# First expert: the fifth unit's parts made before the rows' copies and the gates, the gate by tanh, the slot marks turned by TensorE and copied by ScalarE

## The reference

```python
def moe_swiglu(h, w_router, b_router, w_gate, w_up, w_down):
    t = h.reshape(n_tok, d)                              # 256 x 1024
    logits = (t @ w_router) + b_router                   # 8 experts
    top_v, top_e = lax.top_k(logits, TOP_K)              # TOP_K = 2
    gate = jax.nn.softmax(top_v, axis=-1)
    ...                                                  # rows sorted by expert
    def one(args):                                       # D_FF_EXPERT = 3584
        xb, e = args
        return (jax.nn.silu(xb @ w_gate[e]) * (xb @ w_up[e])) @ w_down[e]
    ...
    y = zeros.at[row_tok].add(out * row_g[:, None])
```

## Time and profile before

| | us |
|---|---|
| median of 3 runs | 2670.47 |
| lowest and highest | 2667.81, 2671.71 |
| the profiled execution's own time | 2667.92 |
| its span | 2666.1 |

### The profile page before, as it was taken

How to read it: one execution, slowest core, us unless ns; L and a number is a source line. 1 busy time by engine, 2 the same in 40 slices (tenths; PEclk the granted TensorE clock), 3 DMA queues, 4 the chain that set the end, 5 groups by cost and what they waited for, 6 DMA issues and landing times.

```text
span 2666.1 us, 65659 instructions
## 1 busy us (share of the span) xinstructions
PE 2564.8 (96%) x27832; PEld 2159.6 (81%) x27832; DVE 1957.1 (73%) x1886; ACT 1614.5 (61%) x1688; POOL 378.9 (14%) x440
## 2 busy tenths in 40 slices
PE   9999999999999999999999999999999999999998
PEld 8887788888887888898788888789777687786775
DVE  5467575565567765666775566798999999999997
ACT  4345664353356654455654445657888787888876
POOL 3214022122115222103022103031000000000000
PEclk9999999999999999999999999998999999999999
DMA  8574365555554555654465665478999999999996
GB/s 270 169 208 131 104 198 197 168 188 189 163 152 152 192 176 178 197 166 141 138 200 200 174 197 166 123 261 338 410 420 422 418 411 422 415 419 418 411 421 274
DMA packets 354985, 666.18 MB, mean 250 GB/s; under 512 B 24545, under 2 KB 285825, under 8 KB 315825
## 3 DMA queue, kind: packets, MB, share of 16 engines
q1 hardware_dynamic: 353920, 661.39, 68.9%
q0 software_dynamic: 528, 0.63, 0.3%
q10 hardware_dynamic: 288, 0.59, 0.1%
HBM read 661.49 MB, written 1.05 MB: 249 GB/s over the span
## 4 chain that ended last, share of the span: by engine, by line
PE 60%; DVE 20%; DMA 7%; ACT 6%; issue 4%; DVEq 2%; POOLq 0%; ACTq 0%; SPq 0%; POOL 0%
PE ps L2331 17%; PE ps L2333 17%; PE ps L2332 17%; DVE w_lo L1619 7%; DMA w<-in_moe_units 3%; DVE w_lo L1459 3%; DVE work L1619 2%; DVE ff L1619 2%; DMA mix<-in_moe_units 2%; ACT w_hi L955 2%; ACT w_hi L846 2%; DMA squares_and_low<-in_moe_units 1%; PE ps L2374 1%; PE ps L2380 1%; PE ps L2375 1%
## 5 line engine op out<-in xcount | busy, mean ns | idle before, releaser
L2331 PE MATMUL ps<-x_hi,w_hi 128*128 128x96 f16 (+2 forms) x5024 | 1077.0, 246 | 26.5 <-DVE w_lo L1619 6.6
L2333 PE MATMUL ps<-x_hi,w_lo 128*128 128x96 f16 (+2 forms) x5024 | 1076.3, 246 | 5.2 <-issue 5.1
L2332 PE MATMUL ps<-squares_and_low,w_hi 128*128 128x96 f16 (+2 forms) x5024 | 1076.4, 246 | 5.0 <-issue 4.9
L1459 DVE SCALAR_TENSOR_TENSOR w_lo<-w,w_hi 128x2048 f16<-128x2048 f32 (+3 forms) x335 | 693.9, 2082 | 295.1 <-ACT w_hi L846 293.4
L846 ACT ACTIVATE w_hi<-w 128x2048 f16<-128x2048 f32 (+3 forms) x335 | 556.8, 1671 | 85.6 <-PE ps L2333 74.8
L2331 PEld LDWEIGHTS ps<-x_hi,w_hi 128*128 128x128 f16 x5024 | 493.1, 98 | 82.8 <-issue 22.0
L2332 PEld LDWEIGHTS ps<-squares_and_low,w_hi 128*128 128x128 f16 x5024 | 492.8, 98 | 51.8 <-issue 7.0
L2333 PEld LDWEIGHTS ps<-x_hi,w_lo 128*128 128x128 f16 x5024 | 492.8, 98 | 48.4 <-issue 6.2
L2332 PE MATMUL ps<-ff,w_hi 128*128 128x272 f16 (+1 forms) x880 | 243.3, 276 | 0.0
L2333 PE MATMUL ps<-ff,w_lo 128*128 128x272 f16 (+1 forms) x880 | 243.3, 276 | 0.0
L2331 PE MATMUL ps<-ff,w_hi 128*128 128x272 f16 (+1 forms) x880 | 243.3, 276 | 0.0
(11 more groups left out here) (408 smaller groups left out, 4772.7 us busy)
## 6 DMA issues: line engine op xcount, KB each, us to landing
w<-in_ffn_w_up_units SPq DMA_DIRECT2D x176, 512.0 KB, 4.6
w<-in_moe_units SPq DMA_DIRECT2D x75, 1024.0 KB, 12.0
w<-in_moe_units SPq DMA_DIRECT2D x56, 1280.0 KB, 15.5
w<-in_w_in SPq DMA_DIRECT2D x112, 512.0 KB, 4.7
mix<-in_moe_units SPq DMA_DIRECT2D x50, 1024.0 KB, 12.0
mix<-in_moe_units SPq DMA_DIRECT2D x36, 1280.0 KB, 15.7
w<-in_mix_w_in SPq DMA_DIRECT2D x60, 512.0 KB, 4.9
squares_and_low<-in_moe_units SPq DMA_DIRECT2D x26, 1024.0 KB, 11.9
```

The source lines that it names most:

```text
L1459: vec.scalar_tensor_tensor(k.w_lo[:, s, 0:size], k.w32[:, s, 0:size], WS, k.w_hi[:, s, 0:size], ALU.mult, ALU.subtract).then_inc(k.parts_r ...
L2331: pe.matmul(acc, w_hi, x_hi, start=first, stop=False)
L2332: pe.matmul(acc, w_hi, x_lo, start=False, stop=False)
L2333: return pe.matmul(acc, w_lo, x_hi, start=False, stop=last)
```

## The change

Four edits, all for the first expert (the later rounds, which run only when an expert has over 96 tokens, follow suit):

- ScalarE makes unit 4's high part ahead of `take_high` instead of between the two copies.
- VectorE makes unit 4's low part right behind unit 3's, ahead of the gates; the gate is made from Tanh(x / 2) by two multiply-adds instead of from Exp by an addition, a reciprocal and a product. ScalarE loads Silu's table ahead of the Tanh.
- The turned marks are no longer made from spread ranks: TensorE turns `to_slot` itself by 16 matmuls with the identity (`turn_marks`, behind unit 3), and ScalarE copies the 96 x 2048 result (`take_marks`, at its step 5). `spread_ranks`, `take_ranks`, `sel16` and the constant `slot_col` go.
- GpSimd loads 14 constants instead of 15.

```diff
-RANKS_SPREAD, RANKS_TAKEN, GATES_SUMMED, GATES_TAKEN, SUM_BEGUN = 1, 3, 9, 11, 15
+MARKS_TURNED, MARKS_TAKEN, GATES_SUMMED, GATES_TAKEN, SUM_BEGUN = 3, 5, 9, 11, 15
-N_CONST = 15
+N_CONST = 14
...
+            if first and u == MARKS_TAKEN:
+                take_marks(0)
...
+    def take_marks(r):
+
+        act.wait_ge(k.marks_turned, r + 1)
+        act.activation(k.to_token[0:CAP, 1:1 + EXPERTS, :], halves(k.ps[0:CAP, TURNED[r]:TURNED[r] + 4, :]), ACT.Copy).then_inc(k.choice_ready, 1)
+
+    expert_split(0, 4, 0)
     take_high(0, 0)
-    expert_split(0, 4, 0)
     take_low(0, 2)
-    act.activation(k.warm2[:, :], k.eps[:, 0:1], ACT.Exp)
+    act.activation(k.warm[:, :], k.eps[:, 0:1], ACT.Silu)
     act.wait_ge(k.lg_ready, 1)
-    act.activation(k.rt[:, :, 1], k.rt[:, :, 0], ACT.Exp).then_inc(k.lg_exped, 1)
-    act.activation(k.warm[:, :], k.eps[:, 0:1], ACT.Silu)
+    act.activation(k.rt[:, :, 1], k.rt[:, :, 0], ACT.Tanh, scale=0.5).then_inc(k.lg_exped, 1)
...
-    vec.tensor_tensor(k.sel[:, :, :], k.member[:, :, :], ranks, ALU.mult)
-    vec.tensor_tensor(k.sel16[:, :, :], k.member[:, :, :], ranks, ALU.mult).then_inc(k.sel_ready, 1)
+    vec.tensor_tensor(k.sel[:, :, :], k.member[:, :, :], ranks, ALU.mult).then_inc(k.sel_ready, 1)
...
-    for u in range(3, E_AHEAD):
+    for u in range(3, E_AHEAD + 1):
         expert_split(0, u, 0)
...
-        vec.tensor_scalar(k.rt[:, :, 2], k.rt[:, :, 1], 1.0, None, ALU.add)
-        vec.drain()
-        vec.reciprocal(k.rt[:, :, 3], k.rt[:, :, 2])
-        vec.drain()
-        vec.tensor_tensor(k.rt[:, :, 4], k.rt[:, :, 1], k.rt[:, :, 3], ALU.mult)
+        vec.tensor_scalar(k.rt[:, :, 3], k.rt[:, :, 1], -0.5, 0.5, ALU.mult, ALU.add)
+        vec.tensor_scalar(k.rt[:, :, 4], k.rt[:, :, 1], 0.5, 0.5, ALU.mult, ALU.add)
...
-    def take_ranks(r):
-        vec.wait_ge(k.sel_spread, r + 1)
-        vec.tensor_scalar(k.to_token[:, 1:1 + EXPERTS, :], halves(k.ps[:, SPREAD[r]:SPREAD[r] + 4, :]), -float(CAP * r), k.slot_col[:, 0:1],
-                          ALU.add, ALU.is_equal).then_inc(k.choice_ready, 1)
...
-            if first and u == RANKS_TAKEN:
-                take_ranks(0)
...
-    def spread_ranks(r):
-
+    def turn_marks(r):
+
+        pe.wait_ge(k.slots_marked, r + 1)
         for e in range(EXPERTS):
             for t in range(2):
-                a = pe.matmul(k.ps[:, SPREAD[r] + e // 2, (e % 2) * T2 + t * P:(e % 2) * T2 + (t + 1) * P],
-                              k.sel16[:, t, e:e + 1].broadcast_to([P, P]), k.ident16[:, :], start=True, stop=True)
-        a.then_inc(k.sel_spread, 1)
+                a = pe.matmul(k.ps[0:CAP, TURNED[r] + e // 2, (e % 2) * T2 + t * P:(e % 2) * T2 + (t + 1) * P],
+                              k.to_slot[:, t, e, :], k.ident16[:, :], start=True, stop=True)
+        a.then_inc(k.marks_turned, 1)
...
-            if first and u == RANKS_SPREAD:
+            if first and u == MARKS_TURNED:
                 pe.wait_ge(k.ident16_made, 1)
-                spread_ranks(0)
+                turn_marks(0)
             if first and u == GATES_SUMMED:
                 pe.wait_ge(k.gates_split, 1)
-                pe.wait_ge(k.slots_marked, 1)
                 sum_gates(0)
```

More of the change, by code:

```diff
@@ L92 @@
 SUM_ADDED = 1
-SPREAD = (4, 0, 0)
+TURNED = (4, 0, 0)
 ROWS_BANK, LOGITS_BANK, ROW_SUMS_BANK, RANKS_BANK, FILLER_BANK = 4, 0, 1, 3, 2
 FILLERS = 4
-RANKS_SPREAD, RANKS_TAKEN, GATES_SUMMED, GATES_TAKEN, SUM_BEGUN = 1, 3, 9, 11, 15
+MARKS_TURNED, MARKS_TAKEN, GATES_SUMMED, GATES_TAKEN, SUM_BEGUN = 3, 5, 9, 11, 15
 GATE_SCALE = 2.0 ** 14
@@ L493, in allocate @@
     k.sel = sb("sel", [P, 2, EXPERTS], F32)
-    k.sel16 = sb("sel16", [P, 2, EXPERTS], F16)
     k.gates16 = sb("gates16", [P, 2, EXPERTS, 2], F16)
@@ L501, in allocate @@
     k.slots = sb("slots", [P, P], F32)
-    k.slot_col = sb("slot_col", [P, 1], F32)
     k.ms = sb("ms", [P, 2, 5], F32)
@@ L621, in allocate @@
     k.sel_ready = sem("sel_ready")
-    k.sel_spread = sem("sel_spread")
+    k.marks_turned = sem("marks_turned")
     k.first_marked = sem("first_marked")
@@ L1418, in moe_round @@
             expert_split(r, u, r * EXPERTS)
+        take_marks(r)
         take_high(r * EXPERTS, 0)
@@ L2071, in vec_program @@
     split_gates()
-    def take_ranks(r):
-        vec.wait_ge(k.sel_spread, r + 1)
-        vec.tensor_scalar(k.to_token[:, 1:1 + EXPERTS, :], halves(k.ps[:, SPREAD[r]:SPREAD[r] + 4, :]), -float(CAP * r), k.slot_col[:, 0:1],
-                          ALU.add, ALU.is_equal).then_inc(k.choice_ready, 1)
     def take_gates(r):
-        sums = k.ps[:, SPREAD[r], :]
+        sums = k.ps[:, TURNED[r], :]
         vec.wait_ge(k.gates_summed, r + 1)
@@ L2118, in take, with split_rest @@
                                          k.d_hi[0:CAP, :], ALU.mult, ALU.subtract).then_inc(k.down_ready, 1)
-        expert_units(lambda u: expert_split(r, u, q), take, last)
+        def split_rest(u):
+            if not (first and u == E_AHEAD):
+                expert_split(r, u, q)
+        expert_units(split_rest, take, last)
     for e in range(EXPERTS):
@@ L2130, in moe_round @@
         for e in range(EXPERTS):
-            mark(e, r)
-        take_ranks(r)
+            a = mark(e, r)
+        a.then_inc(k.slots_marked, 1)
         take_gates(r)
@@ L2230, in pool_program @@
                  (k.slots[:, :], i["c_slots"].broadcast_to([P, P])),
-                 (k.slot_col[:, :], i["c_slots"].rearrange("a s -> s a")),
                  (k.rb[:, :], i["moe_b_router_2"].broadcast_to([P, EXPERTS])),
@@ L3023, in sum_gates @@
             for t in range(2):
-                a = pe.matmul(k.ps[0:CAP, SPREAD[r], 2 * e:2 * e + 2], k.to_slot[:, t, e, :], k.gates16[:, t, e, :], start=t == 0, stop=t == 1)
+                a = pe.matmul(k.ps[0:CAP, TURNED[r], 2 * e:2 * e + 2], k.to_slot[:, t, e, :], k.gates16[:, t, e, :], start=t == 0, stop=t == 1)
         if r == 0:
             for t in range(2):
-                a = pe.matmul(k.ps[:, SPREAD[r], 2 * EXPERTS:3 * EXPERTS], k.ones[:, :], k.member[:, t, :], start=t == 0, stop=t == 1)
+                a = pe.matmul(k.ps[:, TURNED[r], 2 * EXPERTS:3 * EXPERTS], k.ones[:, :], k.member[:, t, :], start=t == 0, stop=t == 1)
         a.then_inc(k.gates_summed, 1)
@@ L3157, in moe_round @@
         else:
-            spread_ranks(r)
+            turn_marks(r)
             sum_gates(r)
```

## The result

The changed kernel took 2673.93 us (median of 12 runs), the kernel before 2667.82 us in the 12 runs that stand beside it: a ratio of 1.0017, 95% interval 1.0009 to 1.0024. It is slower by 0.17%, about 4.5 us by the ratio (the two medians lie 6.1 apart). The forecast was 2.7 us less, and 2673.93 lies above the range of 2663.5 to 2671.5. The forecast's 2667.8 had been worked out from the 2670.47 of three runs, 2.65 above the median of the twelve. The profiled execution has a span of 2672.7 us, 6.6 more than before.

What follows compares the result with a forecast made beforehand. Weights arrive at a fixed saturated rate, so only an earlier start of that stream, fed by VectorE, is kept. 1.3 plus 1.1 to 1.73 gave 2.7 us, 2670.5 - 2.7 = 2667.8 us, range 2663.5 to 2671.5.

Steps and rivals of the forecast that it cites:

- Part 2: VectorE's unit 4 before the gates: the load it frees goes out about 5.3 us earlier, which alone is not kept.
- Part 1: ScalarE's unit 4 before the rows' high copy: TensorE starts the first expert 1.73 us earlier, 1.1 to 1.73 lasting.
- Part 3: Marks turned by TensorE, copied by ScalarE in 1.9 us: VectorE begins unit 10 sooner by 1.3 beyond TensorE's shift.
- the forecast's 1822: Profile time in us at or after which TensorE, behind unit 3, was expected to ask for GpSimd's marks.
- d: TensorE's lasting shift at the first expert, 1.1 to 1.73 us, depending on when the clock rises.
- The sum: 1.3 + 1.1 = 2.4 or 1.3 + 1.73 = 3.0, taken as 2.7 us in all.
- That the shift is kept: VectorE's shift at unit 10 was to last through the saturated weight stream to the end, 2.7 us.
- Swallowed: Rival: something other than VectorE's issues begins the saturated stream; gain 0 to 1 us, some 2670; chance 0.15.
- The prediction's own sign: ScalarE's first wait for a landing was to come 2.7 us sooner; its absence despite unit 10's shift would refute.
- More than the sum: Rival: the copy hides and the load freed 5.3 us earlier is partly kept; 5 to 7 us gained; chance 0.14.
- The table switch: Rival: Silu's table reload of 1.28 us lies before block 0's Silu on ScalarE; 2669; chance 0.04.
- Slower: Rival: lower rate in the saturated stream, 1900 to 2640; 0.8% less makes over 0.2% slower, near 2676; chance 0.05.

Runs made afterwards that it cites:

- act_unit4_first: The kernel before with one edit, ScalarE makes unit 4's high part ahead of both row copies; ratio to the kernel before 0.9993.
- late_turn: The changed kernel with marks turned behind unit 7 instead of 3, ScalarE's copy at step 9, gates' sum behind unit 11; ratio to the kernel before 1.0000.
- vector_marks: The changed kernel with all 14 marks of experts 1 to 7 made by VectorE, none by GpSimd; ratio to the kernel before 0.9991.
- split_marks: The changed kernel with experts 1 to 3 marked by VectorE (6 marks), 4 to 7 by GpSimd (8 marks); ratio to the kernel before 0.9995.
- marks_memset: The changed kernel with GpSimd's 14 marks replaced by memsets of the same outputs, so only its time counts; ratio to the kernel before 0.9994.
- ranks_spread: The changed kernel without its third part: ranks spread behind unit 1 and compared by VectorE, as before; ratio to the kernel before 0.9989.
- copy_late: The changed kernel with all marks on VectorE and ScalarE's copy of the turned marks at step 7 instead of 5; ratio to the kernel before 0.9987.
- the four kernels named above: split_marks, marks_memset, copy_late and split_copy_late, which lose 3.1, 3.1, 2.3 and 1.8 us of their lead between units 20 and 40.
- split_copy_late: The changed kernel with marks split between VectorE (6) and GpSimd (8) and ScalarE's copy at step 7 instead of 5; ratio to the kernel before 0.9985.
- gates_first: The changed kernel with VectorE's unit 4 moved back behind the gates; ratio to the kernel before 1.0017.

## Why the prediction was wrong

**The step that failed** is in Part 2, on GpSimd: "A second such low part now falls in its stretch: it would end near 1818.4 instead of 1815.7 ... so this costs nothing." I had seen the mark of 3199 ns beside unit 3 and counted one more like it. The runs showed that a low part holds GpSimd's marks for its whole length, that between two that stand back to back GpSimd is at times not let in at all (5858 and 5670 ns span two), and that the marks had ended early because VectorE idled 3.0 us for the Exp and then did gates for 2.2. Part 1 took most of that away, alone too (19.8 us in act_unit4_first). late_turn shows the hold going on as long as the low parts do; vector_marks, split_marks and marks_memset show that the pause goes when the marks are in time. GpSimd ended 22.4 us after expert 0's mark, not 12.6, and Part 3 had moved the reading of the marks from behind unit 9 to behind unit 3, at 13.9 (the forecast's 1822 is 16.2 us after the mark; even then the marks would have been 6 us late). Each of the two is harmless alone: ranks_spread has late marks read late, split_marks early marks read early.

The Trainium skill states this rule ("SBUF — State Buffer", section "SBUF: two separate sides"): the port pair that VectorE and GpSimd share is an exclusive lock held for the whole instruction, and a VectorE operation with two SBUF inputs takes it against a GpSimd operation that reads SBUF. By that rule each of units 3 to 8 would hold GpSimd's marks for as long as it ran. The traces agree: 2901 to 5858 ns for marks of 520, and 173 ns for the two memsets beside unit 3.

**Part 1** was right in kind. TensorE began the expert 3.56 us after the mark instead of 5.89: 2.33 sooner, not 1.73, because in this execution the gathers already ran at 2.4 GHz. d, measured at ScalarE's unit 5, was 3.2 to 3.9 us in nine of these profiles and 1.0 in one, copy_late, where the clock rose late; in the profile before it had risen late too. The forecast's 1.1 to 1.73 took that late clock as given, and copy_late's 1.0 is what became of the 1.1. By the ratio the first part is worth 0.07%, 1.9 us, which lies nearer to my d than to the profiles', but its interval reaches 4.3 us and holds both.

**Part 2**, VectorE's side: the load behind unit 4 went out 7.21 us after the mark instead of 12.54, 5.3 sooner as said; the gates took 1.7 us (2.2 less 0.5); one table load, none for Tanh. **Part 3**: copy 1.86 for 1.9; unit 10 in vector_marks 4.32 sooner, of which 3.2 are d, and in marks_memset 5.27, of which 3.9 are d: 1.1 and 1.4 for the forecast's 1.3. **The sum** would thus probably have held, had the marks been in time, but the times don't settle it: vector_marks is 0.09% faster, 2.4 us, for the 2.7 forecast, with an interval from 0 to 4.8 us, and marks_memset 0.06%, 1.6 us, with one from 1.1 slower to 4.0 faster.

**That the shift is kept** held in the changed kernel, and in act_unit4_first, ranks_spread and vector_marks, but not in the four kernels named above. In the changed kernel unit 10 was 5.41 us late, unit 40 5.42, and ScalarE's last high part 5.64. The end shows 2 us more: there ScalarE waited 9.27 us for TensorE's last unit instead of 7.21, which is not explained.

**The rivals.** "Swallowed" is refuted for act_unit4_first, ranks_spread and vector_marks, which keep 3 to 5 us to the end; where a lead shrank, the cause is open. The prediction's own sign, ScalarE's first wait for a landing, came 102.0 us after the mark before, 99.2 in act_unit4_first, and only at 124 to 131 in marks_memset, copy_late and split_copy_late. "More than the sum" didn't come: past d, unit 10 gained the 1.1 to 1.4 of Part 3 and no more. The table switch didn't come. "Slower" came true, but by another mechanism than the one named: from 1900 to 2640 the rate was 415 to 420 GB/s in both kernels. That rival's sum was also off: 760 us at 0.8% less are 6.1 us, and less the gain of 2.7 that is 3.4 us slower, 0.13% and not over 0.2%. What would have shown it beforehand was the question behind a moved wait: not only whether GpSimd's work is done by then in the trace of before, but what let it be done.

## What to carry to other kernels

When a wait is moved ahead, or an idle stretch closed, work out anew when the producer will be done with the new neighbours beside it: here 14 short GpSimd instructions had lived on VectorE's idle time. A recorded duration far above its group's median (3199 ns against 522) was waiting here, so ask what ended it and how often that will now stand there. If GpSimd's work gates something within such a stretch, give it to the engine that would block it (here 2.59 us of VectorE's time for 22 us of GpSimd's) or keep the wait where it was. And before shifts of a few us are compared between single profiles, compare the granted clock in them: here 1.5 us hung on it.

## What the runs showed of the hardware

A GpSimd instruction that reads SBUF doesn't slow down beside VectorE's instructions with two operands from SBUF, it stops: 520 ns become 2.9 us or 5.7 to 5.9 us. In the gap between two such VectorE instructions it may be let in or not; of the four such gaps between units 3 and 8 in the changed kernel two passed without. The low part of the rows, whose one operand comes from PSUM, doesn't hold it: marks take 517 ns beside it (1805.3 to 1806.3). The profile counts the waiting as busy time, so GpSimd looks 22 us busy with 14 marks and no wait is listed on it.

TensorE's pause of 8.6 us took the granted clock from 2.4 to 1.2 GHz (0.55 mean over the window from 1820), and it stayed low into the first matmuls after it; about 2 of the 6.3 us at unit 9 are due to that. Of the changed kernel's 12 runs, nine lie between 2671.5 and 2675.7 us and three between 2667.9 and 2668.6; gates_first, with the same pause, shows the same two groups. split_copy_late, without a pause, has two as well, four runs from 2661.0 to 2661.7 and seven from 2664.6 to 2666.2. What puts a run into one or the other is open.
